# A two-block transformer on one core: the modulation rows that the first layer's feed-forward hosts, computed on VectorE, ScalarE and GpSimd instead of on TensorE

## The reference

```python
    s_lat = jax.nn.silu(c)
    s_ctx = jax.nn.silu(c_ctx)
    for l in range(DEPTH):
        mx = (s_lat @ ada_w[l] + ada_b[l]).reshape(bsz, N_MOD, 1, d)     # N_MOD = 9, d = 1024
        mc = (s_ctx @ ada_w[l] + ada_b[l]).reshape(N_MOD, d)
        x = x + 0.5 * mx[:, 2] * swiglu(ada_norm(x, norm_g[l, 0], mx[:, 0], mx[:, 1]), ffn_w_in[l, 0], ffn_w_out[l, 0])
        hctx = hctx + 0.5 * mc[2] * swiglu(ada_norm(hctx, norm_g[l, 0], mc[0], mc[1]), ffn_w_in[l, 0], ffn_w_out[l, 0])
        ...
```

## Time and profile before

| | us |
|---|---|
| median of 3 runs | 2314.61 |
| lowest and highest run | 2306.75 and 2321.34 |
| span of the profiled execution, first to last instruction | 2314.2 |
| busy in it: TensorE | 2227.1 |
| busy in it: VectorE | 1145.4 |
| busy in it: ScalarE | 846.8 |
| busy in it: GpSimd | 176.3 |

### The profile page before, as it was taken

The page is one execution under the profiler, slowest core; times in us unless marked ns, Lnnn a source line. Parts: engine busy times, 40 slices in busy tenths (PEclk is TensorE's granted clock), DMA queues, the critical chain, the costliest instruction groups (busy, mean ns, idle before and its releaser), DMA issues. The chain is left out here.

```text
span 2314.2 us, 46991 instructions
## 1 busy us (share of the span) xinstructions
PE 2227.1 (96%) x19320; PEld 2091.2 (90%) x19320; DVE 1145.4 (49%) x1930; ACT 846.8 (37%) x1384; POOL 176.3 (8%) x150
## 2 busy tenths in 40 slices
PE   6999999899999999998999999999999999999998
PEld 5986798799999999976999999999999998979998
DVE  5227375653433445456653333454343446487665
ACT  4226454632221233248432222243232234455444
POOL 0003112100000010501200000010000010001000
PEclk9999999999999999999999999999999999999999
DMA  9853544445676244520354666242233233225573
GB/s 297 234 167 86 172 133 104 128 147 154 186 216 186 86 131 117 149 80 28 102 175 141 190 207 189 84 126 85 81 114 94 86 96 101 74 82 146 168 202 112
DMA packets 515900, 315.76 MB, mean 136 GB/s; under 512 B 16035, under 2 KB 513274, under 8 KB 515622
## 3 DMA queue, kind: packets, MB, share of 16 engines
q1 hardware_dynamic: 515160, 313.45, 46.1%
q10 hardware_dynamic: 590, 0.16, 0.0%
HBM read 312.50 MB, written 1.06 MB: 135 GB/s over the span
## 5 line engine op out<-in xcount | busy, mean ns | idle before, releaser
L1118 PE MATMUL ps<-h_hi,w_hi 128*128 128x256 f32 x3376 | 728.0, 280 | 3.5 <-DVE h_lo L1726 1.7
L1118 PE MATMUL ps<-h_lo,w_hi 128*128 128x256 f32 x3376 | 720.6, 278 | 0.0
L1118 PE MATMUL ps<-h_hi,w_lo 128*128 128x256 f32 x3376 | 720.6, 278 | 0.0
L1118 PEld LDWEIGHTS ps<-h_hi,w_hi 128*128 128x128 f32 x3376 | 537.8, 189 | 22.9 <-issue 21.6
L1118 PEld LDWEIGHTS ps<-h_lo,w_hi 128*128 128x128 f32 x3376 | 539.4, 189 | 0.1
L1118 PEld LDWEIGHTS ps<-h_hi,w_lo 128*128 128x128 f32 x3376 | 537.9, 189 | 0.0
L1960 DVE TENSOR_TENSOR w_lo<-stage,w_hi 128x1024 fp32r<-128x1024 f32 x227 | 285.0, 1258 | 441.5 <-ACT w_hi L1467 440.9
L1467 ACT ACTIVATE w_hi<-stage 128x1024 fp32r<-128x1024 f32 x227 | 236.6, 1055 | 334.4 <-PE ps L1118 200.4
L1960 DVE TENSOR_TENSOR w_lo<-deep,w_hi 128x1024 fp32r<-128x1024 f32 x184 | 226.1, 1234 | 226.9 <-ACT w_hi L1467 225.2
L1467 ACT ACTIVATE w_hi<-deep 128x1024 fp32r<-128x1024 f32 x184 | 191.9, 1055 | 179.7 <-PE ps L1118 141.4
L1118 PE MATMUL ps<-g_hi,w_hi 128*128 128x256 f32 x1100 | 232.9, 280 | 0.2
(11 more groups left out here) (413 smaller groups left out, 2858.0 us busy)
## 6 DMA issues: line engine op xcount, KB each, us to landing
modw<-in_ada_w SPq DMA_DIRECT2D x72, 1024.0 KB, 6.7
stage<-in_ffn_w_in SPq DMA_DIRECT2D x88, 512.0 KB, 3.9
deep<-in_ffn_w_in SPq DMA_DIRECT2D x88, 512.0 KB, 3.9
modw<-in_w_mod SPq DMA_DIRECT2D x18, 1024.0 KB, 6.1
stage<-in_w_in SPq DMA_DIRECT2D x30, 512.0 KB, 5.3
stage<-in_ffn_w_out SPq DMA_DIRECT2D x32, 384.0 KB, 3.5
stage<-in_even_w_in SPq DMA_DIRECT2D x24, 512.0 KB, 4.0
deep<-in_ffn_w_out SPq DMA_DIRECT2D x32, 384.0 KB, 3.4
```

The source lines that it names most:

```text
L1118: last = mm(ps[:, j, v - a:v - a + SEQ], w_part[wp][:, u % RING, c, :], x_part[xp][:, x, v:v + SEQ], start=first and wp == xp and v == a, ...
```

## The change

For the 26 pairs in these gemms the product with the two vectors leaves TensorE. A pair's 512 columns are loaded as one tile `modw2` (two DMAs of four row chunks each, `sp_pair`). For the first vector VectorE multiplies each of the 8 row chunks (128 partitions x 512) by that chunk's column of `svec` and accumulates (`dve_pair_summed`: one tensor_scalar, seven scalar_tensor_tensor, each waiting for the one before). For the second vector ScalarE scales each chunk (`act_pair_scaled`) and GpSimd adds them up (`pool_pair_summed`, seven adds; three scratch tiles between the two). TensorE then only sums over the partitions: `pe_pair_rows`, 4 matmuls of 256 columns for a pair, with a stationary piece `pick` that places each sum on a partition of its own. Bias, transposes and reduction stay.

The places change as well. In an up turn (hper 2) VectorE has chunks 0 to 2 at place 0, 3 to 5 at place 1, 6 and 7 at place 2; ScalarE has chunks 0 to 3 at place 0 and 4 to 7 at place 1; TensorE's sums stand behind unit 2 and the transposes inside unit 3. In a down turn (hper 4) the two pairs follow each other through the places. At the start of these gemms VectorE and ScalarE wait for the last norm to be done, since the accumulators lie in its memory.

The core of the diff:

```diff
+        FETCHED = {2: {3: 0}, 4: {1: 0, 3: 1}}
+        SCALED = {2: {0: [(0, 0, 4)], 1: [(0, 4, 8)]}, 4: {0: [(0, 0, 6)], 1: [(0, 6, 8), (1, 0, 3)], 2: [(1, 3, 8)]}}
+        SUMMED = {2: {0: [(0, 0, 3)], 1: [(0, 3, 6)], 2: [(0, 6, 8)]}, 4: {0: [(0, 0, 5)], 1: [(0, 5, 8), (1, 0, 2)], 2: [(1, 2, 8)]}}
+        GATHERED = {2: {(2, 7): 0}, 4: {(1, 10): 0, (3, 4): 1}}
+        TURNED = {2: {(3, 3): 0}, 4: {(2, 3): 0, (3, 8): 1}}
+        BIASED_FIRST, BIASED_LAST, KEPT = {2: {3: 0}, 4: {2: 0}}, {2: {}, 4: {3: 1}}, {2: {3: 0}, 4: {2: 0, 3: 1}}
...
+        def sp_pair(eng, p, i, pair):
...
+            for h in range(2):
+                rows = slice(4 * h, 4 * h + 4)
+                eng.wait_ge(S("mod_scaled"), at["mod_scaled"] - KC + 4 * (h + 1))
+                eng.wait_ge(S("mod_acc0"), at["mod_acc0"] - KC + 4 * (h + 1))
+                eng.dma_start(modw2[:, rows, :], w[:, rows, bass.ds(first, 2 * SEG)]).then_inc(mod_full[h], 16)
...
+        def pe_pair_rows(eng, p, i, pair, rounds):
+
+            at, sums = pair_counts(p, i, pair), pair_buffers(p, pair)[0]
+            eng.wait_ge(S("mod_acc0"), at["mod_acc0"] + KC)
+            eng.wait_ge(S("mod_acc1"), at["mod_acc1"] + KC - 1)
+            eng.wait_ge(S("mod_sum"), at["mod_sum"])
+            for n in range(2):
+                for v in range(2):
+                    q = 2 * n + v
+                    last = mm(ps[32 * q:32 * q + 32, 4, 0:SEG], pick[:, 3 - q:35 - q], sums[:, v, n * SEG:(n + 1) * SEG],
+                              start=True, stop=True, skip_group_check=True)
+            up(last, "mod_rows", rounds, by=2)
...
+        def act_pair_scaled(eng, p, i, pair, k0, k1, rounds):
...
+                elif k > 3:
+                    eng.wait_ge(S("mod_acc1"), at["mod_acc1"] + k - 3)
+                up(act(sums[:, 1, :] if k == 0 else scaled_w[(k - 1) % 3], modw2[:, k, :], ACT.Copy, scale=svec[:, m["block"], k, 3:4]), "mod_scaled", rounds)
...
+        def dve_pair_summed(eng, p, i, pair, k0, k1, rounds):
...
+                if k == 0:
+                    eng.wait_ge(S("mod_rows"), at["mod_rows"] - 2 * pair)
+                    ins = V.tensor_scalar(total_, modw2[:, 0, :], svec[:, m["block"], 0, 2:3], None, ALU.mult)
+                else:
+                    eng.wait_ge(S("mod_acc0"), at["mod_acc0"] + k)
+                    ins = V.scalar_tensor_tensor(total_, modw2[:, k, :], svec[:, m["block"], k, 2:3], total_, ALU.mult, ALU.add)
...
+        def pool_pair_summed(eng, p, i, pair, rounds):
+
+            at, total_ = pair_counts(p, i, pair), pair_buffers(p, pair)[0][:, 1, :]
+            for k in range(1, KC):
+                eng.wait_ge(S("mod_scaled"), at["mod_scaled"] + k + 1)
+                if k > 1:
+                    eng.wait_ge(S("mod_acc1"), at["mod_acc1"] + k - 1)
+                up(nc.gpsimd.tensor_tensor(total_, total_, scaled_w[(k - 1) % 3], ALU.add), "mod_acc1", rounds)
...
-            if chained(p):
-                pair_rows(0, 0, 1)
...
-                    pair = pair_behind(p, j, js) if chained(p) else None
-                    if pair is not None:
-                        pe_cols(eng, p, i, k["hper"], 2 * pair + 1, rounds)
-                        if 2 * pair + 2 < k["hper"]:
-                            pair_rows(i, pair + 1, rounds)
-                        elif rounds > 1 or i < k["n"] // step - 1:
-                            pair_rows(i + 1, 0, rounds)
```

More of the change, by code:

```diff
@@ L200, in modvec @@
         add("modvec", {"mod_ready": 1}, block=block, l=l, parts=parts, which=which)
-    add("setup", {"rows_T": 1, "rows_sb": 1, "s_ready": 2})
+    add("setup", {"rows_T": 1, "rows_sb": 1, "s_ready": 2, "mod_scaled": KC, "mod_acc0": KC, "mod_acc1": 1})
     add("load", {"tokens_T": KC, "rms_ready": 2, "diag_ready": 2, **{f"bank_free{b}": 1 for b in range(8)}})
@@ L265, in ffn @@
             if (l, i) == (0, 0):
-                add("head", {"unit_done": 4, "w_hi": 4, "w_ready": 4, "c_done": 2, **{f"bank_free{b}": 1 for b in range(4)}, "ms_sum": 2, "rms_ready": 2,
+                add("head", {"unit_done": 4, "w_hi": 4, "w_ready": 4, "x_done": 2, **{f"bank_free{b}": 1 for b in range(4)}, "ms_sum": 2, "rms_ready": 2,
                              "diag_ready": 2, "rstd_ready": 2, "added": 4, "presq": 4, "pre_added": 2, **HALF_H,
@@ L763, in sp_gemm @@
                         if k["evac"] in ("swiglu", "resid"):
-                            ready = {(2, 1): (0, 1), (4, 0): (0, 1), (4, 2): (2, 3)}.get((k["hper"], j), ()) if len(js) == step and s == per - 1 else ()
-                            for x in ready:
-                                sp_segment(eng, p, i, k["hper"], x)
+                            pair = pair_work(FETCHED, p, js, j) if s == per - 1 else None
+                            if pair is not None:
+                                sp_pair(eng, p, i, pair)
                         elif k["hper"] and len(js) == step and s == 0:
@@ L1000, in pe_head @@
                             pe_half_rstd(eng, p, 0, 1)
-                    up(last, "c_done") if half else up(last, "unit_done", by=2)
+                    up(last, "x_done") if half else up(last, "unit_done", by=2)
                 if half:
@@ L1133, in product @@
                         last = chunk(j, u, c, x, s + n == 0, s == per - 1 and n == kc - 1)
-                    up(last, "unit_done", rounds)
+                        if n == kc - 1:
+                            up(last, "unit_done", rounds)
+                        pair = pair_work(GATHERED, p, js, (j, sum(ks[:s]) + n))
+                        if pair is not None:
+                            pe_pair_rows(eng, p, i, pair, rounds)
+                        pair = pair_work(TURNED, p, js, (j, sum(ks[:s]) + n))
+                        if pair is not None:
+                            pe_pair_cols(eng, p, i, pair, rounds)
             def product_pair(i, rounds):
@@ L1506, in act_gemm @@
                             act_split(eng, u0 + i * turn + x)
+                    for pair, k0, k1 in pair_work(SCALED, p, js, j) or ():
+                        act_pair_scaled(eng, p, i, pair, k0, k1, rounds)
                     if k.get("decays") in ("k", 0, 1):
@@ L2024, in dve_gemm @@
                             dve_split(eng, u0 + i * turn + x)
+                    for pair, k0, k1 in pair_work(SUMMED, p, js, j) or ():
+                        dve_pair_summed(eng, p, i, pair, k0, k1, rounds)
+                    pair = pair_work(BIASED_LAST, p, js, j)
+                    if pair is not None:
+                        dve_pair_biased(eng, p, i, pair, rounds)
+                    pair = pair_work(KEPT, p, js, j)
+                    if pair is not None:
+                        dve_cols(eng, p, i, k["hper"], 2 * pair + 1, rounds)
                     if not narrow:
@@ L2099, in pool_gemm @@
             k = p.kw
+            if in_pairs(p):
+                for i, js, rounds in turns(eng, k["n"], k["step"]):
+                    for pair in range(k["hper"] // 2 if len(js) == k["step"] else 0):
+                        pool_pair_summed(eng, p, i, pair, rounds)
             if k["evac"] == "post":
```

120 lines of the change are left out of this document (83 added, 37 removed).

## The result

The changed kernel takes 2524.1 us (median of 4 runs, 2522.0 to 2526.2) beside 2311.7 us for the kernel before (4 runs, 2306.8 to 2321.3): a ratio of 1.091, 95% interval 1.089 to 1.093. It is slower by 9%, some 212 us. The forecast was 2508, with a range of 2400 to 2560.

A forecast was written before the change was run, and what follows sets the result against it. TensorE, busy 96% of the span, was taken to bound the kernel; 2314.2 + 110 (up turns) + 31 (their clock falls) + 53 (down turns) = 2508 us, range 2400 to 2560.

The forecast's parts named there:

- The bound and the gain: Hosting gemms: only TensorE's time counts; a pair falls from 2.18 to 0.81 us, 36 us over 26 pairs at most.
- The wait in the up turns: TensorE waits for VectorE's accumulations from 16.4 to 23.9 us into each up turn, 7.5 us; 18 turns lose 110 us.
- The three alternating accumulations: Up turns: three VectorE accumulations take turns with GpSimd's adds, each 1.1 + 0.75 us.
- the copy: Copy in VectorE's Silu product, possibly held up by GpSimd: 0.3 us a turn, 5 us in all, outside the sum.
- The clock: TensorE's clock falls once behind each up turn's wait, costing 1.7 us, 31 us over 18 turns; down turns add 7.
- Rival (b): TensorE's clock stays up despite the waits: 2470 us, chance 0.12.
- Rival (c): TensorE's clock stays low for twice as long after the waits: 2546 us, chance 0.11.
- Up turns in all: 18 up turns: 110 us from the longer turns and 31 us from the clock.
- Down turns: Each goes from 34.52 to 46.1 us plus one clock fall of 1.7; four turns lose 53 us.
- Other edits at nothing: Three small setup memsets and the waits for the last norm at a gemm's start cost nothing.
- a date for that load: Down turns: the second pair's weights, asked for behind a gemm weight, land at about 24.7 us into the turn.
- Rival (d): VectorE's and GpSimd's sums are ready when TensorE arrives, 16.4 us into an up turn: 36 us won, 2279 us, chance 0.03.

The follow-up runs named there:

- eighth run: Down gemms as before; in up turns VectorE alone makes both vectors' sums at place 0, alternating, transposes three chunks later: 2294.5 us, 0.992 of the kernel before.
- Experiment 1: Changed kernel with GpSimd's seven adds of a pair over 1 column instead of 512: 2423.5 us, 1.045 of the kernel before.
- experiment 2: Changed kernel with VectorE's seven multiply-accumulates of a pair over 1 column instead of 512: 2468.9 us, 1.066 of the kernel before.
- Experiment 4: Changed kernel with 60 unused matmuls on TensorE ahead of its waits for the sums: 2487.4 us, 1.072 of the kernel before.
- fifth run: Changed kernel with the down gemms put back as before, only the 18 up pairs changed: 2456.4 us, 1.063 of the kernel before.
- Experiment 9: Down gemms as before; in up turns VectorE alone makes both vectors' sums, at the change's places 0, 1, 2: 2457.5 us, 1.060 of the kernel before.
- third run: Changed kernel with both GpSimd's adds and VectorE's multiply-accumulates over 1 column, places and loads kept: 2331.6 us, 1.006 of the kernel before.
- sixth run: Changed kernel with TensorE's up-turn sums behind the seventh chunk of unit 3, transposes behind the eighth: 2415.5 us, 1.046 of the kernel before.
- run 11: Not a run: in "of the sixth run 11 had no low stretch" the 11 counts waits of the sixth run.

## Why the prediction was right, and where a size was off

**The bound and the gain.** TensorE alone set the pace, and 1.37 us per pair was to be won. That was right; the eighth run shows it as a turn of 22.8 us. In the changed kernel none of it is visible, since every turn waits.

**The wait in the up turns.** Forecast 7.5 us, released by VectorE; measured 6.7 to 7.0 us from the second turn of each gemm on, released by VectorE. The three alternating accumulations were put at 1.85 each and took 1.72; the two free ones at 0.88 and took 0.77. Against that stands the copy (0.66 instead of 0.43), for which the forecast had 0.3 us in a sentence of its own and nothing in the sum. Experiment 1 shows the alternation as its cause, experiment 2 that the delay lasts as long as the add does, whatever the size of VectorE's operation.

**The clock.** This term was too small: 1.7 us per turn forecast, 2.2 per wait measured. I had taken one stretch of 3.4 us at 0.50 from the earlier trace rows; behind a wait of 7 us the level stays low for 2.9 to 6.3 us of work. In the down turns both waits bring a fall, not one. Experiment 4 gives 51 to 53 us for the whole, where the forecast had 38. Rival (b), the clock stays up, is out. Rival (c), low twice as long, is farther off than the forecast: 4.4 us of low clock is between 3.4 and 6.8, nearer to the first.

**Up turns in all.** 110 + 31 = 141 us forecast; the fifth run, with only the up turns changed, has +145. That this part is so near is luck: the wait was put too long and the clock too short, and the two errors cancel: 22.7 + 7.0 + 2.2 = 31.9 us a turn, beside 22.7 + 7.5 + 1.7.

**Down turns.** 53 us forecast; 65 by the ratios of the fifth and the changed kernel, 58 by their traces. A turn was put at 46.1 + 1.7 and took 49.2 to 49.8. The waits were not too short: by the forecast's own times TensorE waits 7.5 and 6.8 us, and it waited 7.3 and 6.0 in the turn shown, 12.0 to 13.5 for the two together in all four. What the sum lacks is the second fall of the clock, and the size of each: twice 2.2 us in place of 1.7. The alternation was counted rightly: five of the six accumulations in the row of 668.72 stand beside an add (9.29 us for the six), the last one is free.

**Other edits at nothing.** Ahead of the hosting stretches the two profiles agree: TensorE is busy for 451.2 us of the first 495 in both.

**What the prediction did not see** is the part that a remedy needs. It said that VectorE's chain of five accumulations, a product and a split could not be in time, and put the blame on both the place and the alternation with GpSimd. Experiment 9 shows that at this place the alternation is not needed for the loss: what counts is the work behind the second split, whoever does it. With GpSimd's columns taken away but the place kept (1), half of the loss stays, and with all columns taken away (3) a wait of 1.3 us still eats the gain. The third run also shows something that the forecast had not seen in the down turns: the first pair's bias stands in VectorE's order behind the second pair's first product, and so behind its load. The forecast had a date for that load, 24.7 us into the turn, but not this place of the bias. Rival (d), the faster one, named 16.4 us as the point from which it decides; that point was right, and the eighth kernel meets it by moving the work in front of the split (over at 557.86, asked for at 558.8).

What stays open: the eighth kernel's down gemms are those of before. VectorE has, by the durations above, 8 splits (9.8 us), four residual additions (3.5) and, for two pairs, 32 operations (21) for a turn of 32 us; that does not fit, but one pair of the two might, if its load is there in time. It was not tried.

## What to carry to other kernels

Work that is moved off the engine that sets the pace has a date by which it must be back; look for the place in the other engine's order where its inputs are there and nothing that waits for the pace-setter stands in front of it. The busy shares (49% here) say only that such a place may exist. Two engines that hold each other up are a poor division of labour; here one of them, with two independent chains that alternate, was faster. And a wait of 7 us on TensorE costs 9 here, since the clock takes 2 more.

## What the runs showed of the hardware

- A VectorE operation of one column with two SBUF inputs takes 0.24 us alone and 1.33 us beside GpSimd's adds (1.29 us each alone); one of 512 columns 0.75 and 1.72.
- VectorE's fp32 copy of 512 columns is held up as well: 0.43 us alone, 0.66 and 0.87 where an add is under way.
- GpSimd is held up in turn: its adds take 1.6 to 1.7 us beside VectorE's accumulations, 1.29 alone. In the group of the one-column adds they still take 0.57 to 0.68 us each, which I had not expected.
- Two chains of accumulations that alternate on VectorE start every 0.66 us; a single chain through a semaphore starts every 0.77.
- Behind 6.9 us without work TensorE's clock is at 1.2 GHz before the work begins and stays there for 2.9 to 6.3 us of it; waits of 1.3 us (third run) left the clock up; of the 16 waits of 1.8 to 2.2 us in the up turns of the sixth run 11 had no low stretch behind them, the other five one of 3.3 to 3.4 us of work.
